# The first modulations of a two-layer transformer kernel, taken in pairs of k-tiles between the tiles of the first projection

## What is computed

```
sh_a, sc_a, ga_a, sh_f, sc_f, ga_f = split(silu_c @ w_mod + b_mod, 6)        # latent tokens
tsh_a, tsc_a, ...                  = split(silu_ct @ w_mod + b_mod, 6)       # context tokens
h  = rms_norm(x,  g_attn) * (1 + sc_a)  + sh_a
ht = rms_norm(xt, g_attn) * (1 + tsc_a) + tsh_a
q, k, v of three head groups = h @ w_in,  ht @ w_in
```

## Time and profile before

| | us |
|---|---|
| median of 3 runs | 1866.49 |
| range | 1864.91 to 1866.91 |
| the profiled execution | 1864.14 |
| its span in the profile | 1862.3 |
| PE busy | 1745.9 (94% of the span) |
| DVE / ACT / POOL busy | 914.6 / 484.3 / 862.5 |

### The profile page before, as it was taken

One profiled execution on the slowest core, in us unless ns is written; L12 is line 12 of the kernel. 1 busy time (PEld: TensorE's weight loads), 2 busy tenths in 40 slices (PEclk: granted clock), 3 DMA queues, 4 the chain that ended last, 5 costly groups with the idle time before them and its releaser, 6 DMA issues.

```text
span 1862.3 us, 30083 instructions
## 1 busy us (share of the span) xinstructions
PE 1745.9 (94%) x11175; PEld 1475.2 (79%) x11175; DVE 914.6 (49%) x1615; ACT 484.3 (26%) x984; POOL 862.5 (46%) x671
## 2 busy tenths in 40 slices
PE   5899979987989999999999998998887999999998
PEld 3588868976878888888888887887776778888886
DVE  2525478886355461255315455456996633123122
ACT  2212267775120100000000012224775121010010
POOL 0234337884324544444444453542021566666664
PEclk9999989999999999999999998998998999999999
DMA  8234444432114432334223322443200323333332
GB/s 293 46 91 115 114 120 120 132 92 57 57 38 132 124 102 68 102 114 122 80 80 112 116 65 46 113 110 100 50 2 1 91 79 94 98 92 100 92 94 96
DMA packets 316392, 174.42 MB, mean 94 GB/s; under 512 B 87550, under 2 KB 307598, under 8 KB 316302
## 3 DMA queue, kind: packets, MB, share of 16 engines
q1 hardware_dynamic: 288608, 148.54, 28.7%
q10 hardware_dynamic: 27694, 24.66, 4.2%
HBM read 159.04 MB, written 2.83 MB: 87 GB/s over the span
## 4 chain that ended last, share of the span: by engine, by line
PE 79%; DVE 12%; issue 3%; DMA 2%; POOL 2%; ACT 2%; SPq 1%; ACTq 0%; DVEq 0%; POOLq 0%
PE acc L746 66%; DVE prob_t L1550 3%; DVE stat L1536 3%; PE side L705 1%; PE mod_ps L818 1%; DVE o_sum L1562 1%; PE side L912 1%; PE small L988 1%; POOL split_w L569 1%; PE small L927 1%; PE acc L895 1%; PE acc L896 1%; PE mod_ps L716 1%; DVE stat L1543 1%; PE small L838 1%
## 5 line engine op out<-in xcount | busy, mean ns | idle before, releaser
L746 PE MATMUL acc<-act,split_w 128*128 128x512 f32 x5088 | 1006.3, 358 | 22.3 <-DVE act L1377 16.3
L746 PEld LDWEIGHTS acc<-act,split_w 128*128 128x128 f32 x5088 | 835.5, 190 | 171.6 <-issue 15.9
L569 POOL TENSOR_TENSOR split_w<-raw_w,split_w 128x1024 fp32r<-128x1024 f32 (+1 forms) x220 | 519.7, 2362 | 18.4
L566 POOL TENSOR_SCALAR split_w<-raw_w 128x1024 fp32r<-128x1024 f32 (+1 forms) x220 | 228.8, 1040 | 315.0 <-PE acc L746 205.2
L746 PE MATMUL acc<-hidden,split_w 128*128 128x512 f32 (+1 forms) x1584 | 308.8, 357 | 0.2 <-DVE hidden L1619 0.2
L746 PEld LDWEIGHTS acc<-hidden,split_w 128*128 128x128 f32 x1584 | 261.7, 188 | 46.0 <-DVE hidden L1619 0.6
L565 POOL TENSOR_TENSOR turnstile<-ones 128x1 f32<-128x1 f32 x136 | 53.6, 394 | 454.9 <-PE acc L746 454.9
L1617 DVE TENSOR_TENSOR prod<-acc,silu_g 128x768 f32<-128x768 f32 (+1 forms) x44 | 36.3, 824 | 331.1 <-PE acc L746 331.1
L1397 DVE SCALAR_TENSOR_TENSOR x_t<-acc,mod,x_t 128x512 f32 (+1 forms) x96 | 60.6, 659 | 258.4 <-PE acc L746 258.4
L1261 ACT ACTIVATE silu_g<-acc 128x768 f32<-128x768 f32 (+1 forms) x44 | 31.1, 706 | 455.3 <-PE acc L746 455.3
L1199 ACT ACTIVATE prob<-acc,stat,score_scale 128x768 f32<-128x768 f32 (+5 forms) x160 | 130.9, 818 | 57.1 <-DVE stat L1543 55.0
(11 more groups left out here) (164 smaller groups left out, 1568.2 us busy)
## 6 DMA issues: line engine op xcount, KB each, us to landing
raw_w<-in_w_gate SPq DMA_DIRECT2D x44, 512.0 KB, 3.9
raw_w<-in_w_up SPq DMA_DIRECT2D x44, 512.0 KB, 3.8
mod_chunk<-in_w_mod ACTq DMA_DIRECT2D x22, 1024.0 KB, 5.3
raw_w<-in_w_mod SPq DMA_DIRECT2D x36, 512.0 KB, 3.9
raw_w<-in_w_in SPq DMA_DIRECT2D x64, 256.0 KB, 3.7
raw_w<-in_w_down SPq DMA_DIRECT2D x32, 512.0 KB, 4.0
mod_start<-in_w_mod SPq DMA_DIRECT2D x4, 2048.0 KB, 12.6
ks<-q_split SPq DMA_DIRECT2D x64, 96.0 KB, 2.2
```

Source lines behind the costliest of these rows:

```text
L566: pool.tensor_scalar(split_w[slot][:, 0, 0:n, :], raw_w[slot][:, 0:n, :], 1.0, 0.0, ALU.mult, ALU.add).then_inc(hi_w, 1)
L569: pool.tensor_tensor(split_w[slot][:, 1, 0:n, :], raw_w[slot][:, 0:n, :], split_w[slot][:, 0, 0:n, :].bitcast(F32), ALU.subtract).then_inc ...
L746: mm = pe.matmul(acc[slot][:, a:b], split_w[slot][:, part == 2, k, :], moving[:, part == 1, k, a:b], start=(k == 0 and part == 0), stop=(k ...
```

## The change

The first modulations are cut another way. A group i now holds the 256 shift columns and the 256 scale columns of k-tiles 2i and 2i + 1 (`START_TILES` = 2), loaded by two DMAs of 256 columns each; so a group is all that two k-tiles of the activations need. There are four buffers instead of three; the fourth lies over `tokens`, so its load waits until all tokens are transposed. `turn_first_modulations(i)` turns the four 128-column pieces of one group, and DVE's `modulations(i)` forms shift and gain for two k-tiles. Group 0 is computed ahead of the sums of squares as before and turned behind them, group 1 follows the spreading of the inverse, and groups 2 and 3 stand between the k-tiles of the pair: a new callback `in_tile(k)` puts turning 1, 2, 3 ahead of k-tiles 1, 3, 5 and groups 2 and 3 ahead of k-tiles 2 and 4. ACT copies group k/2 + 1 ahead of the high part of k-tiles 0, 2 and 4. ACT loads its square-root table ahead of the squares, in layer 0 too.

The seven constants, the zeros and the `rpb` copy move from ACT's DMA queue to SP's, and SP doesn't wait for the vectors any more ahead of `w_mod`. The identity has a semaphore of its own. All else is as it was.

```diff
-        mod_start = [place(f"mod_start{i}", [P, 8, 4 * P], F32, a0 + i * 16384) for i in range(3)]
+        mod_start = [None] * N_START
...
+        for i, where in enumerate((a0, b0 + 24576, b0 + 47104, b0)):
+            mod_start[i] = place(f"mod_start{i}", [P, 8, 4 * P], F32, where)
...
-            sp.wait_ge(vecs_in, N_VECS * 16)
-            for i in range(MOD_FIRST // 4):
-                if i >= 3:
-                    sp.wait_ge(mod_start_done, i - 2)
-                sp.dma_start(mod_start[i % 3][:, :, :],
-                             w_mod[0, :, 512 * i:512 * i + 512].rearrange("(k p) n -> p k n", p=P)
-                             ).then_inc(mod_start_in[i % 3], 16)
+            def load_start(i):
+
+                n = START_TILES * P
+                for s in range(2):
+                    sp.dma_start(mod_start[i][:, :, s * n:s * n + n],
+                                 w_mod[0, :, D * s + n * i:D * s + n * i + n].rearrange("(k p) n -> p k n", p=P)
+                                 ).then_inc(mod_start_in[i], 16)
+
+            for i in range(N_START - 1):
+                load_start(i)
+            for dst, src in ((pair_ones, k_pairs), (swap, k_swap), (cos, k_cos), (sin, k_sin)):
+                sp.dma_start(dst[:, :], src[:, :]).then_inc(consts_in, 16)
+            sp.dma_start(window32[:, :, :], k_window[:, :, :]).then_inc(consts_in, 16)
+            sp.dma_start(columns[:, :, :], k_columns[:, :, :]).then_inc(consts_in, 16)
+            sp.dma_start(sinks[:, :], bass.AP(sink.tensor, 0, [[0, P], [1, DEPTH * 6]])).then_inc(consts_in, 16)
+            sp.wait_ge(xt_ps, KT)
+            load_start(N_START - 1)
+
+            n_rows = DEPTH * 4 * 15
+            sp.wait_ge(zeros_set, 1)
+            sp.dma_start(bias_dram.rearrange("a (b c) -> a b c", c=64), zeros[0:n_rows, :, :].broadcast_to((n_rows, 12, 64))).then_inc(zero_in, 16)
...
+                    if u == 1:
+                        sp.wait_ge(zero_in, 16)
+                        sp.dma_start(bass.AP(bias_dram.tensor, 1, [[768, n_rows], [49, 16], [1, 31]]),
+                                     bass.AP(rpb.tensor, 0, [[31, n_rows], [0, 16], [1, 31]])).then_inc(bias_rows_in, 16)
...
+            pe.wait_ge(ident_in, 16)
...
-                pe.wait_ge(mod_start_in[i % 3], 16 * (i // 3 + 1))
-                if i >= 2:
-                    pe.wait_ge(mod_rows_ready, i - 1)
-                ps = (small, mod_ps)[i % 2]
+                pe.wait_ge(mod_start_in[i], 32)
+                if i:
+                    pe.wait_ge(mod_rows_ready, i)
                 for k in range(KT):
-                    mm = pe.matmul(ps[0:2, :], silu_c[:, k::KT], mod_start[i % 3][:, k, :],
+                    mm = pe.matmul(small[0:2, :], silu_c[:, k::KT], mod_start[i][:, k, :],
                                    start=(k == 0), stop=(k == KT - 1))
                 mm.then_inc(mod_start_done, 1)
+
+            def turn_first_modulations(i):
+
+                pe.wait_ge(mod_rows_ready, i + 1)
+                if i:
+                    pe.wait_ge(mod_ready, i)
+                for a in range(2 * START_TILES):
+                    mm = pe.transpose(mod_ps[:, 2 * a:2 * a + 2], mod_rows[:, 512 * i + P * a:512 * i + P * a + P], ident[0:2, 0:2])
+                mm.then_inc(mod_first, 1)
...
                     first_modulations(0)
                 sum_squares(2 * l, TOK)
                 if l == 0:
-                    for i in range(1, MOD_FIRST // 4):
-                        first_modulations(i)
-
-                    pe.wait_ge(mod_rows_ready, MOD_FIRST // 4)
-                    for m in range(MOD_FIRST):
-                        mm = pe.transpose(mod_ps[:, 2 * m:2 * m + 2], mod_rows[:, P * m:P * m + P], ident[0:2, 0:2])
-                    mm.then_inc(mod_first, 1)
+                    turn_first_modulations(0)
                 spread_inverse(2 * l, TOK)
+                if l == 0:
+                    first_modulations(1)
+
+                def in_tile(k):
+                    if l == 0 and k in (1, 3, 5):
+                        turn_first_modulations((k + 1) // 2)
+                    if l == 0 and k in (2, 4):
+                        first_modulations(k // 2 + 1)
+                    pe.wait_ge(h_lo, 2 * l * KT + k + 1)
...
-                            dense_pair(TOK, lambda k: pe.wait_ge(h_lo, 2 * l * KT + k + 1))
+                            dense_pair(TOK, in_tile)
...
-            for dst, src in ((pair_ones, k_pairs), (swap, k_swap), (cos, k_cos), (sin, k_sin)):
-                sc.dma_start(dst[:, :], src[:, :]).then_inc(consts_in, 16)
-            sc.dma_start(window32[:, :, :], k_window[:, :, :]).then_inc(consts_in, 16)
-            sc.dma_start(columns[:, :, :], k_columns[:, :, :]).then_inc(consts_in, 16)
-            sc.dma_start(sinks[:, :], bass.AP(sink.tensor, 0, [[0, P], [1, DEPTH * 6]])).then_inc(consts_in, 16)
-
-            sc.wait_ge(zeros_set, 1)
-            n_rows = DEPTH * 4 * 15
-            sc.dma_start(bias_dram.rearrange("a (b c) -> a b c", c=64), zeros[0:n_rows, :, :].broadcast_to((n_rows, 12, 64))).then_inc(zero_in, 16)
-            sc.wait_ge(zero_in, 16)
-            sc.dma_start(bass.AP(bias_dram.tensor, 1, [[768, n_rows], [49, 16], [1, 31]]),
-                         bass.AP(rpb.tensor, 0, [[31, n_rows], [0, 16], [1, 31]])).then_inc(bias_rows_in, 16)
...
+            def shifted(nu, l, w, ahead=None):
 
                 for k in range(KT):
+                    if ahead:
+                        ahead(k)
                     sc.wait_ge(scaled_ready, nu * KT + k + 1)
...
-                if l:
-                    sc.activation(root_first[:, :], eps[:, 0:1], ACT.Sqrt)
+                if l == 0:
+                    sc.wait_ge(filled, 2)
+                sc.activation(root_first[:, :], eps[:, 0:1], ACT.Sqrt)
                 squares(2 * l, TOK, ready)
+
+                def take_rows(i):
+                    sc.wait_ge(mod_start_done, i + 1)
+                    sc.activation(mod_rows[:, 512 * i:512 * i + 512], small[0:2, :], ACT.Copy).then_inc(mod_rows_ready, 1)
+
+                if l == 0:
+                    take_rows(0)
                 take_norm_root(2 * l, TOK)
-                if l == 0:
-                    for i in range(MOD_FIRST // 4):
-                        sc.wait_ge(mod_start_done, i + 1)
-                        sc.activation(mod_rows[:, 512 * i:512 * i + 512], (small, mod_ps)[i % 2][0:2, :],
-                                      ACT.Copy).then_inc(mod_rows_ready, 1)
-                shifted(2 * l, l, TOK)
+                shifted(2 * l, l, TOK, lambda k: take_rows(k // 2 + 1) if l == 0 and k in (0, 2, 4) else None)
...
+                        if u_in(l) + j == 0:
+                            sc.wait_ge(zero_in, 16)
...
+            def modulations(i):
+
+                two = dict(s=2, a=2)
+                k0, k1 = START_TILES * i, START_TILES * (i + 1)
+                b = vecs[:, 0:MOD_FIRST].rearrange("p (s k a) -> p s k a", s=2, a=1)[:, :, k0:k1, :].broadcast_to((P, 2, START_TILES, 2))
+                ps = mod_ps[:, 0:4 * START_TILES].rearrange("p (s k a) -> p s k a", **two)
+                ve.tensor_tensor(mod[:, 0, 0:MOD_FIRST, :].rearrange("p (s k) a -> p s k a", s=2)[:, :, k0:k1, :], ps, b,
+                                 ALU.add).then_inc(mod_ready, 1)
+                ve.wait_ge(mod_ready, i + 1)
+                g = vecs[:, 48 + k0:48 + k1].rearrange("p (m a) -> p m a", a=1).broadcast_to((P, START_TILES, 2))
+                ve.scalar_tensor_tensor(out=gain[:, 0, 0, k0:k1, :], in0=mod[:, 0, KT + k0:KT + k1, :], scalar=1.0, in1=g,
+                                        op0=ALU.add, op1=ALU.mult).then_inc(gain_ready, 1)
+                ve.wait_ge(gain_ready, i + 1)
...
-                if nu == 0:
-                    ve.wait_ge(mod_first, 1)
-                    modulations(0, 0, 0, MOD_FIRST)
-                    ve.wait_ge(mod_ready, 1)
-                    gains(0, 0)
                 ve.wait_ge(inv_spread, nu + 1)
-                ve.wait_ge(gain_ready, [1, 2, 4, 4][nu])
-                if nu == 0:
+                if nu:
+                    ve.wait_ge(gain_ready, N_START + (1 if nu == 1 else 3))
+                else:
                     ve.wait_ge(xt_act, 4)
...
+                    if nu == 0 and k % START_TILES == 0:
+                        if k:
+                            lo(k - 1)
+                        ve.wait_ge(mod_first, k // START_TILES + 1)
+                        modulations(k // START_TILES)
...
-                    if k:
+                    if k and (nu or k % START_TILES):
                         lo(k - 1)
```

14 lines of the change are left out of this document (6 added, 8 removed).

## The result

| | before | after |
|---|---|---|
| median, us | 1866.70 (8 runs) | 1872.59 (8 runs) |
| range, us | 1862.42 to 1870.43 | 1868.51 to 1874.46 |
| ratio, 95% interval | | 1.0031 [1.0018, 1.0044] |
| profiled execution, its span | 1864.14, 1862.3 | 1872.90, 1871.1 |
| PE leaves the pair of units 0 and 1 | 89.55 | 97.36 |

A forecast was written before the change was run, and what follows sets the result against it. PE has 79% of the span, nearly all dense projections; only the head changes. Weights at 48.3 plus 40.0 of tiles plus 6.2 of low clock end the pair at 94.5, 4.95 later: 1864.14 + 4.95 = 1869.1 us, range 1863.5 to 1874.

The forecast's parts named there:

- late weights or longer stretches: SP's loads or half-clock stretches at the start of the pair: longer than forecast, result slower; 42%.
- the pair end: PE leaving units 0 and 1: forecast 94.5 us against 89.55 before, 4.95 later; what follows hangs on it alone.
- I don't add this: Base of the total: the profiled execution was 2.35 us under the median 1866.49, and this was left out.
- The head, up to the scaling: Start of the kernel: transposes done 20.5, additions to 29.7, root 32.7, spreading 34.9, DVE scaling from 35.4 us.
- The weights: SP's single load line: loads through at 37.3, POOL's splits ready at 48.3 us, last to release the first tile.
- the rival: Late weights on SP's line: from 49.4 us on the result passes 1870.2; at 51 it is 1871.8; 40%.
- Bound (a): First tile waiting for PE's group 1, ACT's row copy and DVE's part: 45.2 us, 3.1 ahead of the weights.
- The two waits: PE idle behind groups 2 and 3 while ACT copies rows and tiles are made: about 3.3 us each.
- From the first tile to the pair end: Dense tiles of units 0 and 1 with groups 2 and 3 between: 40.0 us at full clock.
- The clock: Half-clock stretches behind PE's waits in the pair: three cost 6.2 us, ends 3.2 and 9.1.
- The rival that the clock holds altogether: Idling of 3.3 us in the pair doesn't lower the clock: pair end 88.3, result 1862.9; 12%.
- three of three: Trace before the change: all three waits of 3.2 us and over lowered the clock, evidence against the clock holding.

The follow-up runs named there:

- Weights first: The changed kernel with SP's constants and zeros moved behind the weights of units 0 and 1: 1868.95 us, ratio 1.0018, pair end 93.32.
- the change's second execution: The changed kernel run once more, unchanged: 1866.80 us in one run, first tile 50.66, pair end 94.94.
- Rows behind the tiles: The changed kernel with ACT copying rows of groups 1 to 3 behind k-tiles 1, 3, 5: 1864.05 us, ratio 0.9985, pair end 88.15.
- the filled kernel: The changed kernel with idle identity matmuls on PE behind groups 1 to 3, three waits added: 1866.81 us, ratio 1.0005, pair end 93.96.
- these six executions: Changed kernel twice, with 2 KB w_mod rows twice, with constants and zeros behind weights, with DMAs back on ACT: first tile to pair end 44.28 to 46.85 us.
- two groups ahead: The changed kernel with weights first, groups 0 and 1 ahead of the sums, two PSUM banks, later row copies: 1851.41 us, ratio 0.9926.

## Why the prediction was off where it was

The forecast was 1869.1 with 46% for "within 0.2%"; 1872.59 came, inside the range 1863.5 to 1874.0, and what came is the case that had 42%, slower by late weights or longer stretches. By its steps:

**The method held.** Forecast: all turns on the pair end, what follows hangs on it alone. Measured: 7.8 of 8.8 us, with what follows known to a few us only.

**The base is the step that put the forecast on the wrong side of the edge.** The sum was made on the profiled execution, 1864.14, which lay 2.35 us under the median, and "I don't add this" left the forecast at 1869.1, while the edges of no change were laid around the median, 1862.8 and 1870.2. A shift of 4.95 us is 0.27%: by its own size already slower. Against the median it would have read 1871.4, over the edge. The measured shift of the medians is 5.9 us (interval 3.4 to 8.2), of which the sum had 4.95. The mechanism and most of the size were right; forecast and edges stood on different bases. Between the pair ends of the two profiles the sum had 4.95 and 7.8 came: 2.2 of the missing 2.9 us are the late weights, 0.65 the way from the first tile to the end of the pair (46.85 against 40.0 + 6.2).

**The head, up to the scaling, was right.** Transposes done: forecast 20.5, measured 21.0. Additions 23.4 to 29.7, measured 23.83 to 30.1. Root 32.7, measured 33.09. Spreading ended 34.9, measured 36.6, since it ran at half clock (2.93 us instead of 1.60); scaling 35.4 (35 to 37), measured 37.0. All of it lay under the weights, as the text said.

**The weights were the mis-sized term.** Forecast 48.3 (the terms as printed add up to 37.2 and not 37.3, so 48.2), measured 50.25 and, again, 50.24. The loads ended about 1.5 us later: 8.39 MB at 375 GB/s are 22.4 us, at the 348 GB/s of the stretch 24.1. The 375 was read over 2 us of a later load; why the rate was lower here, no run shows. The splits took 7.40 instead of 6.9 us: the second's high part took 1.49 instead of 1.04 while DVE made the low parts of the first tiles. So the first tile started 2.2 us late. This passes 49.4, the point that the text gave for the rival. The forecast went by the rate of 1 KB rows, 6% under that of 2 KB rows; 348 against 383 to 385 GB/s is 9%. The Trainium skill, "DMA: Bandwidth & Descriptors", section Specifications, has line rate from 512 bytes on; the traces disagree with it here.

**Bound (a) was right, and only just covered.** Weights first, with the weights out of the way, starts at 47.08. The forecast of (a) was 45.2; of the 1.9 us between, 1.3 are the spreading at half clock (2.93 for 1.60). In the change's second execution, where sums and spreading were slow together, PE's first tile was released by DVE at 50.66, when the weights had been ready for 0.4 us.

**The two waits were right in kind and nearly in size:** 3.3 us forecast, 2.87 measured, twice, ended by DVE. Rows behind the tiles shows that their cause is ACT's order: with that one edit both are gone.

**From the first tile to the pair end** the forecast had 40.0 at full clock, and the filled kernel measured 40.8. **The clock:** 6.2 us forecast from three stretches, 6.0 measured in the profiled execution, 3.5 in the next, so that the first comes so near is partly luck. The ends, 3.2 and 9.1, hold all six. The rival that the clock holds altogether did not come in any execution, but "three of three" waits of 3.2 us and more was too small a sample for "always": of the twelve waits of 2.87 us in these six executions, three passed without a fall. The trace of before had more rows for it than the text read: three shorter waits, 2.89 us up to 277.06, 2.23 up to 1298.87 and 2.48 up to 1485.00, each with the clock at 0.50 behind it, and a fourth of 3.66 us, up to 1133.72, into which PE went at 0.50 already. They speak for the fall, as the forecast had it.

**Not weighed at all:** that the interleaving could be kept and its cost removed. The text named ACT's row copy as the cause of both waits, so it could have said that a copy one step later takes 9 us away.

## What to carry to other kernels

When work is cut into pieces to start a consumer earlier, look at what stands in each engine's queue ahead of the piece that the consumer waits for: here a copy of 0.59 us on ACT, which waited for a group of PE, uncovered two waits of 2.87 us and the half clock behind them, and one place later it cost nothing. Put such producer work where PE waits anyway (two groups ahead, with the weights first and the rows behind, is 13 us faster than the kernel before; 5.6 of these are beyond the other two edits). And lay the forecast and the edges of "no change" on the same base: a shift added to one profiled execution is compared with that execution, not with a median.
